# Expert blocks of a mixture of experts: the store of a block's rows moved from the sync engine's queue to ScalarE's

## The chip, the cores and the metric

One core of one Trainium2 chip runs the whole program. The metric is the device time of one execution in microseconds. The program was run three times, and the median is what counts. One execution was also taken with the hardware profiler; its trace is what the text reads.

## The reference, cut to what matters

The reference is one layer of a hybrid backbone over 9 tiles of 128 tokens (1 of a prompt, 8 of a sample): a mixer (attention beside a state-space scan), a mixture of experts, a final norm. Only the experts matter here. Each token takes one group of four experts and in it the two best, so each token is worked on by two experts of 16:

```python
hidden = (jax.nn.silu(jnp.einsum('nd,edf->nef', hf, lw['w_exp_gate']))
          * jnp.einsum('nd,edf->nef', hf, lw['w_exp_up']))
y = jnp.einsum('nef,efd->nd', hidden * combine.astype(hf.dtype)[..., None], lw['w_exp_down'])
```

The model width is 1024, an expert's inner width is 256. So an expert has 2 MB of gate and up weights and 1 MB of down weights in float32.

## The kernel before

**Blocks.** The routing stage sorts the (token, expert) pairs by expert into 33 blocks of 128 rows, each block with one expert (`BLOCKS`). `block_expert`, `block_new` and `block_buf` hold, for each block, its expert, whether that expert differs from the one of the block before, and which of two buffers holds its raw weights. `expert_stage` runs over the blocks: the rows of a block are gathered from HBM (`xg`), turned on TensorE (`x_ps`), split in a high and a low part (`xT_hi`, `xT_lo`), multiplied with gate and up weights that are split in the same way (three matmuls for each product, 24 of 512 columns for a block), passed through SiLU and the routing weight (`hid`), turned and split again (`hidT_hi`, `hidT_lo`), and multiplied with the split down weights (12 matmuls). The result `y_ps` is copied to `y` in SBUF and stored to `y_slots` in HBM, from where the final stage gathers it.

**Engines.** Each engine runs its own `body(t, left)` for each block t. A body works on several blocks at once:

- The sync engine (SP) issues the loads. `load_gu(t+3)` reads three values (expert, buffer, whether new) from SBUF into registers, waits until VectorE has split the gate and up weights of block t+1 (`gu_lo_done`), and issues two loads of 1 MB. Then comes `store(t-1)`: it waits until ScalarE has copied `y` of block t-1 (`y_read`) and issues the store of 512 KB. Then `load_d(t+2)`: three values, a wait for GpSimd's split of block t's down weights, and a load of 1 MB. A load whose expert is not new is skipped (`cond=new`), but it counts on its semaphore.
- ScalarE (ACT) copies the high parts of the turned rows (`x_high`, two halves), does the SiLU, casts the gate and up weights to their high parts in four pieces (`gu_high(t+3)`, two before and two after `evacuate(t)`), evacuates `y_ps` (`evacuate(t)`), and casts the down weights (`d_high(t+2)`). It works in this written order. The first piece of `gu_high(t+3)` waits for the two loads.
- VectorE (DVE) makes the low parts of the gate and up weights, of the rows and of the hidden rows. GpSimd (POOL) makes the low part of the down weights (`d_low`), and issues the gathers.
- TensorE (PE) runs `gate_up(t+1)` in two halves around the turns, and the down product of block t.

`evacuate(t)` waits for the store of the block before: `act.wait_ge(y_out, t.n * 16 + 16)`.

Of the kernel before, what the change touches and what calls it, by code (L numbers as in the profile page):

```python
# [15 lines left out]
P = 128  # L16
# [26 lines left out]
BLOCKS = 2 * TILES + NE - 1  # L43
# [1997 lines left out]
def expert_stage(nc, I, C, W, M):  # L2041
# [5 lines left out]
    with ExitStack() as ctx:  # L2047
# [9 lines left out]
        y = s.sb("y", [P, D])  # L2057
        x_ps, gu_ps, h_ps, y_ps = s.ps("x", D), [s.ps(f"gu{u}") for u in range(2)], s.ps("h"), s.ps("y", D)
        gu_in, d_in, xg_in = ([s.sem(f"{k}{u}") for u in range(2)] for k in ("gu_in", "d_in", "xg_in"))
        y_out = s.sem("y_out")  # L2060
# [5 lines left out]
        hidT_done, y_done, y_read = (s.sem(k) for k in ("hidT_done", "y_done", "y_read"))  # L2066
# [3 lines left out]
        def blocks(eng, body):  # L2070

            assert BLOCKS % 2 == 1
            body(Step(0, 0), 4)
            with eng.Fori(0, (BLOCKS - 5) // 2) as i:
                body(Step(i, 1), 4)
                body(Step(i, 2), 4)
            for n in range(BLOCKS - 4, BLOCKS):
                body(Step(0, n), BLOCKS - 1 - n)

        def weight_buffer(eng, k):  # L2080

            return eng.value_load(W["block_buf"][0:1, bass.ds(k.n, 1)], min_val=0, max_val=1)

        def block_values(eng, k):

            return (eng.value_load(expert[0:1, bass.ds(k.n, 1)], min_val=0, max_val=NE - 1), weight_buffer(eng, k),
                    eng.value_load(W["block_new"][0:1, bass.ds(k.n, 1)], min_val=0, max_val=1))

        @block.sync
        def _(sp):  # L2090
            def load_gu(k):
                e, buf, new = block_values(sp, k)
                sp.wait_ge(gu_lo_done, k.n + 1)
                sp.dma_start(wgu[:, buf, :, 0:FF], I["w_exp_gate"][0, e].rearrange("(k p) f -> p k f", p=P), cond=new).then_inc(gu_in[k.buf], 16)
                sp.dma_start(wgu[:, buf, :, FF:], I["w_exp_up"][0, e].rearrange("(k p) f -> p k f", p=P), cond=new).then_inc(gu_in[k.buf], 16)

            def load_d(k):
                e, buf, new = block_values(sp, k)
                sp.wait_ge(d_lo_done, k.n + 1)
                sp.dma_start(wd[:, buf], I["w_exp_down"][0, e].rearrange("(k p) d -> p k d", p=P), cond=new).then_inc(d_in[k.buf], 16)  # L2100

            def body(t, left):
                if left >= 3:
                    load_gu(t.next().next().next())
                if left == 1:
                    sp.wait_ge(gu_lo_done, BLOCKS + 2)
                    load_final_gains(sp, I, W, M)
                if not (isinstance(t.n, int) and t.n == 0):
                    store(Step(t.i, t.c - 1))
                if left >= 2:  # L2110
                    load_d(t.next().next())

            def store(t):
                sp.wait_ge(y_read, t.n + 2)
                sp.dma_start(M["y_slots"][bass.ds(t.n * P, P), :], y[:]).then_inc(y_out, 16)

            load_gu(Step(0, 0))
            load_d(Step(0, 0))
            load_gu(Step(0, 1))
            load_d(Step(0, 1))  # L2120
            load_gu(Step(0, 2))
            blocks(sp, body)
            store(Step(0, BLOCKS - 1))
            sp.wait_ge(y_out, 16 * (BLOCKS + 1))

        @block.gpsimd
# [94 lines left out]
        @block.scalar  # L2221
        def _(act):
            act.sem_inc(y_read, 1)
            act.sem_inc(y_out, 16)

            def gu_high(k, buf, pieces):
                if pieces[0] == 0:
                    act.wait_ge(gu_in[k.buf], k.nth * 32 + 32)
                    act.wait_ge(gu_done, k.n + 1)
                for j in pieces:  # L2230
                    act.copy(wgu_hi[:, k.buf, j:j + 2], wgu[:, buf, j:j + 2]).then_inc(gu_hi_done, 1)  # L2231

            def d_high(k):
                buf = weight_buffer(act, k)
                act.wait_ge(d_in[k.buf], k.nth * 16 + 16)
                act.wait_ge(y_done, k.n + 1)
                act.copy(wd_hi[:, k.buf], wd[:, buf]).then_inc(d_hi_done, 1)  # L2237

            def x_high(k, half):

                act.wait_ge(x_turned, k.n + 3)
                if half == 0:
                    act.wait_ge(gu_half_done, k.n + 1)
                else:
                    act.wait_ge(gu_done, k.n + 2)
                cols = slice(half * 512, (half + 1) * 512)
                act.copy(xT_hi[:, cols], x_ps[:, cols]).then_inc(x_hi_done[half], 1)

            def silu(k):
                act.wait_ge(gu_done, k.n + 3)  # L2250
                act.wait_ge(hid_done, k.n + 2)
                act.activation(act_g[:], gu_ps[k.buf][:, 0:FF], ACT.Silu).then_inc(silu_done, 1)

            def evacuate(t):
                act.wait_ge(y_done, t.n + 3)
                act.wait_ge(y_out, t.n * 16 + 16)
                act.copy(y[:], y_ps[:]).then_inc(y_read, 1)

            def body(t, left):
                if left >= 2:  # L2260
                    x_high(t.next().next(), 0)
                    x_high(t.next().next(), 1)
                if left >= 1:
                    silu(t.next())
                if left >= 3:
                    ahead = t.next().next().next()
                    buf = weight_buffer(act, ahead)
                    gu_high(ahead, buf, range(0, KT // 2, 2))
                evacuate(t)
                if left >= 3:  # L2270
                    gu_high(ahead, buf, range(KT // 2, KT, 2))
                if left >= 2:
                    d_high(t.next().next())

            gu_high(Step(0, 0), weight_buffer(act, Step(0, 0)), range(0, KT, 2))
            d_high(Step(0, 0))
            x_high(Step(0, 0), 0)
            x_high(Step(0, 0), 1)
            gu_high(Step(0, 1), weight_buffer(act, Step(0, 1)), range(0, KT, 2))
            x_high(Step(0, 1), 0)  # L2280
            x_high(Step(0, 1), 1)
            silu(Step(0, 0))
            gu_high(Step(0, 2), weight_buffer(act, Step(0, 2)), range(0, KT, 2))
            d_high(Step(0, 1))
            blocks(act, body)

        @block.vector
# [56 lines left out]
def load_final_gains(sp, I, W, M):  # L2344
    gate0, gate1, gain = final_gains(W)
    for cond, gate in enumerate((gate0, gate1)):
        sp.dma_start(gate, row_bcast(M["mods"][cond, GATE2 * D:(GATE2 + 1) * D])).then_inc(W["final_in"], 16)
    sp.dma_start(gain, row_bcast(I["final_norm_g"])).then_inc(W["final_in"], 16)
# [229 lines left out]
```

## Time and profile before

| | |
|---|---|
| time, median of 3 runs | 1292.05 us (1291.84 to 1296.66) |
| the profiled execution: time, span | 1293.32 us, 1291.6 us |
| expert stage | from about 880 to 1232 us of the span |
| PE, DVE, ACT, POOL busy over the whole span | 89%, 64%, 51%, 36% |
| stores of `y` | 33 of 512 KB, issued by SP |
| new experts' loads | 2 MB + 1 MB each |

The profile counts an engine as busy while a compute instruction of it runs. The issuing of a DMA, a wait and the reading of a value into a register are not busy time; they stand in the trace under the engine's queue (SPq, ACTq). The granted clock of TensorE is given as a share of its upper level (2.4 GHz); 0.50 is the lower one (1.2 GHz). "DMA share" is the mean busy share of the 16 DMA engines.

### The profile page before, as it was taken

How to read it: one execution, taken by the hardware profiler on the slowest of the kernel's cores; microseconds unless marked ns; L12 is line 12 of the kernel's file. 1: busy time of each engine (PE TensorE's matmuls, PEld its weight loads, DVE VectorE, ACT ScalarE, POOL GpSimd, SP SyncE). 2: the span in 40 equal slices, each digit the busy share in tenths (PEclk: the TensorE clock that was granted, in tenths of full speed). 3: DMA queues.
4: the chain of work that ended last, by engine and by line, in shares of the span. 5: the costliest groups of instructions: out<-in, count | busy, mean ns of one | idle time of the engine just before them, and what ended most of it. 6: DMA issues, size and time to landing. Idle time of an engine off the chain costs nothing. (4 is left out here: it accounts for less than half of the span.)

```text
span 1291.6 us, 19584 instructions
## 1 busy us (share of the span) xinstructions
PE 1149.3 (89%) x6100; PEld 952.6 (74%) x6100; DVE 829.2 (64%) x1234; ACT 658.2 (51%) x1085; POOL 466.3 (36%) x272
## 2 busy tenths in 40 slices
PE   4799999988999996988996999946899989899984
PEld 1687777768999885888886888835678777678751
DVE  0764455014564785777775566667889888999737
ACT  2651112114334773666666455416678787688622
POOL 0000000020001682566772000003687877688650
PEclk9899999989999997999998999967999999999988
DMA  9427586421200907236111533225987987633375
GB/s 365 139 106 278 175 293 220 141 68 38 54 1 3 227 34 168 67 85 147 38 50 47 178 105 101 80 99 194 327 268 259 347 312 252 235 143 115 117 261 210
DMA packets 127093, 204.92 MB, mean 159 GB/s; under 512 B 19265, under 2 KB 89825, under 8 KB 124975
## 3 DMA queue, kind: packets, MB, share of 16 engines
q1 hardware_dynamic: 118108, 176.90, 41.6%
q0 software_dynamic: 7344, 26.74, 6.0%
q10 hardware_dynamic: 1570, 0.38, 0.2%
q8 instruction: 39, 0.64, 0.2%
q14 instruction: 32, 0.25, 0.1%
HBM read 215.61 MB, written 45.01 MB: 202 GB/s over the span
## 5 line engine op out<-in xcount | busy, mean ns | idle before, releaser
L88 DVE TENSOR_TENSOR moe_wgu_lo<-moe_wgu,moe_wgu_hi 128x1024 fp32r<-128x1024 f32 x132 | 222.2, 1720 | 38.7 <-issue 19.8
L88 POOL TENSOR_TENSOR moe_wd_lo<-moe_wd,moe_wd_hi 128x1024 fp32r<-128x1024 f32 x66 | 190.2, 2903 | 62.4 <-ACT moe_wd_hi L2237 61.6
L2231 ACT CAST moe_wgu_hi<-moe_wgu 128x1024 fp32r x132 | 131.7, 1050 | 53.9 <-DMA moe_wgu<-in_w_exp_up 53.5
L93 PE MATMUL proj_acc_ps<-proj_w_hi,hidden_hT_hi 128*128 128x512 f32 x288 | 117.6, 408 | 8.0 <-DVE hidden_hT_lo L88 8.0
L93 PE MATMUL moe_gu_ps<-moe_wgu_hi,moe_xT_hi 128*128 128x512 f32 x264 | 110.6, 419 | 15.5 <-DVE moe_xT_lo L88 15.5
L95 PE MATMUL proj_acc_ps<-proj_w_hi,hidden_hT_lo 128*128 128x512 f32 x288 | 115.2, 400 | 0.0
L94 PE MATMUL proj_acc_ps<-proj_w_lo,hidden_hT_hi 128*128 128x512 f32 x288 | 114.7, 398 | 0.0
L1332 POOL TENSOR_TENSOR att_e<-att_e 128x1152 f32<-128x1152 f32 (+1 forms) x36 | 86.0, 2390 | 77.0 <-DVE att_e L1412 77.0
L94 PE MATMUL moe_gu_ps<-moe_wgu_lo,moe_xT_hi 128*128 128x512 f32 x264 | 106.1, 402 | 0.0
L95 PE MATMUL moe_gu_ps<-moe_wgu_hi,moe_xT_lo 128*128 128x512 f32 x264 | 106.1, 402 | 0.0
L1350 ACT ACTIVATE att_e<-att_sc_ps,att_shift 128x1152 f32<-128x1152 f32 (+1 forms) x72 | 81.5, 1132 | 40.1 <-DVE att_shift L1401 39.9
L719 POOL MEMSET conv_ones<- 128x128 f32 x1 | 0.2, 205 | 280.1 <-POOLq L83 280.1
L1401 DVE TENSOR_REDUCE att_shift<-att_sc_ps 128x1 f32<-128x1152 f32 (+1 forms) x72 | 86.1, 1230 | 5.5 <-PE att_sc_ps L1446 5.3
L1475 PE MATMUL att_turned_ps<-att_in_v_tok,att_aT 128*128 128x128 f32 x584 | 77.2, 280 | 8.2 <-ACT att_aT L1358 8.0
L1475 PEld LDWEIGHTS att_turned_ps<-att_in_v_tok,att_aT 128*128 128x128 f32 x584 | 70.0, 192 | 14.1 <-ACT att_aT L1358 10.8
L93 PEld LDWEIGHTS proj_acc_ps<-proj_w_hi,hidden_hT_hi 128*128 128x128 f32 x288 | 54.8, 190 | 27.5 <-DVE hidden_hT_lo L88 8.2
L93 PEld LDWEIGHTS moe_gu_ps<-moe_wgu_hi,moe_xT_hi 128*128 128x128 f32 x264 | 50.7, 192 | 32.2 <-issue 9.6
L373 ACT ACTIVATE proj_halves<-proj_heads_ps 128x512 fp32r<-128x512 f32 x19 | 11.4, 599 | 106.8 <-PE proj_heads_ps L576 63.4
L93 PE MATMUL conv_group_ps<-hidden_hT_hi,conv_w_hi 128*128 128x384 f32 x192 | 65.1, 339 | 0.0
L95 PEld LDWEIGHTS proj_acc_ps<-proj_w_hi,hidden_hT_lo 128*128 128x128 f32 x288 | 54.8, 190 | 13.2
L2237 ACT CAST moe_wd_hi<-moe_wd 128x2048 fp32r x33 | 63.0, 1908 | 2.6 <-DMA moe_wd<-in_w_exp_down 2.5
L95 PE MATMUL conv_group_ps<-hidden_hT_hi,conv_w_lo 128*128 128x384 f32 x192 | 64.2, 334 | 0.0
(376 smaller groups left out, 2831.2 us busy)
## 6 DMA issues: line engine op xcount, KB each, us to landing
moe_wgu<-in_w_exp_gate SPq DMA_DIRECT2D x34, 1024.0 KB
moe_wgu<-in_w_exp_up SPq DMA_DIRECT2D x34, 1024.0 KB
moe_wd<-in_w_exp_down SPq DMA_DIRECT2D x34, 1024.0 KB
scratch_y_slots<-moe_y SPq DMA_DIRECT2D x33, 512.0 KB
proj_raw<-in_w_in SPq DMA_DIRECT2D x32, 256.0 KB, 5.1
proj_feat<-in_w_ada SPq DMA_DIRECT2D x4, 2048.0 KB, 8.6
proj_xh<-in_w_ada SPq DMA_DIRECT2D x4, 2048.0 KB, 9.9
scratch_h<-late_h SPq DMA_DIRECT2D x9, 512.0 KB, 2.9
```

What stands on the lines that cost most here:

```text
L88: return eng.tensor_tensor(low, value, high.bitcast(F32), ALU.subtract)
L93: pe.matmul(out, a_high, b_high, start=start, stop=False)
L94: pe.matmul(out, a_high, b_low, start=False, stop=False)
L95: return pe.matmul(out, a_low, b_high, start=False, stop=stop)
L373: act.activation(halves[:, m % 2, 0], heads_ps[m % 2][:], ACT.Copy, scale=SCALE if m < TILES else 1.0).then_inc(half_high, 1)
L719: pool.memset(ones[:], 1.0).then_inc(zeroed, 1)
L1332: pool.tensor_tensor(e[:, it.e, 0, 0:it.keys], e[:, it.e, 0, 0:it.keys], e[:, it.e, 1, 0:it.keys], ALU.add).then_inc(a_done, 1)
L1350: act.activation(as_banks(it, e[:, it.e, m, 0:it.keys]), scores_of(it, m), ACT.Exp, bias=shift[:, it.e, m:m + 1], accum_out=total[:, it.e, ...
L1401: dve.tensor_reduce(shift[:, it.e, m:m + 1], scores_of(it, m), AX if it.prompt else AXY, ALU.max, negate=True).then_inc(shift_done[m], 1)
L1475: mm = pe.matmul(o_ps, aT[:, j * P:(j + 1) * P], v_tok[:, j + (0 if it.prompt else 1), it.head * P:(it.head + 1) * P], start=(j == 0), sto ...
L2231: act.copy(wgu_hi[:, k.buf, j:j + 2], wgu[:, buf, j:j + 2]).then_inc(gu_hi_done, 1)
L2237: act.copy(wd_hi[:, k.buf], wd[:, buf]).then_inc(d_hi_done, 1)
```

## The change

`store` leaves the sync engine's body and goes into ScalarE's. There it stands in the body of its own block, behind the last two pieces of `gu_high` and ahead of `d_high`, and it goes through ScalarE's own DMA queue. Its wait on `y_read` now is a wait of ScalarE's sequencer for ScalarE's own copy. The sync engine's body holds only the loads. Nothing of the computation, of the buffers or of the bytes moved is changed.

```diff
@@ expert_stage, block.sync @@
                 if left == 1:
                     sp.wait_ge(gu_lo_done, BLOCKS + 2)
                     load_final_gains(sp, I, W, M)
-                if not (isinstance(t.n, int) and t.n == 0):
-                    store(Step(t.i, t.c - 1))
                 if left >= 2:
                     load_d(t.next().next())
-
-            def store(t):
-                sp.wait_ge(y_read, t.n + 2)
-                sp.dma_start(M["y_slots"][bass.ds(t.n * P, P), :], y[:]).then_inc(y_out, 16)
@@
             load_gu(Step(0, 2))
             blocks(sp, body)
-            store(Step(0, BLOCKS - 1))
             sp.wait_ge(y_out, 16 * (BLOCKS + 1))
@@ expert_stage, block.scalar @@
+            def store(t):
+                act.wait_ge(y_read, t.n + 2)
+                act.dma_start(M["y_slots"][bass.ds(t.n * P, P), :], y[:]).then_inc(y_out, 16)
+
             def body(t, left):
@@
                 evacuate(t)
                 if left >= 3:
                     gu_high(ahead, buf, range(KT // 2, KT, 2))
+                store(t)
                 if left >= 2:
                     d_high(t.next().next())
```

## Rows read from the trace of the kernel before

**Rows 1.** The page, its part 1, TensorE.
```profile
PE 1149.3 (89%) x6100; PEld 952.6 (74%) x6100; DVE 829.2 (64%) x1234; ACT 658.2 (51%) x1085; POOL 466.3 (36%) x272
```
**Rows 2.** Windows of the expert stage: busy us of each engine, granted clock, DMA share, GB/s.
```profile
1000.00:1040.00 40.00, 38.06 (x182) 30.44 (x182) 33.04 (x34) 30.66 (x35) 30.64 (x17) 1.00 0.99 356
1080.00:1120.00 40.00, 33.63 (x151) 26.17 (x150) 35.35 (x30) 26.64 (x31) 29.02 (x16) 0.96 0.68 230
1160.00:1200.00 40.00, 40.00 (x194) 32.47 (x193) 37.79 (x38) 33.93 (x39) 33.77 (x18) 1.00 0.30 111
```
**Rows 3.** Timeline of ACT, evacuations of `y`: first, two of steady blocks, last.
```profile
909.33 1.01 ACT L2257 COPY moe_y<-moe_y_ps 128x1024 f32<-128x1024 f32 x1
...
1149.85 1.02 ACT L2257 COPY moe_y<-moe_y_ps 128x1024 f32<-128x1024 f32 x1
...
1216.43 1.02 ACT L2257 COPY moe_y<-moe_y_ps 128x1024 f32<-128x1024 f32 x1 [1.87 <-PE moe_y_ps L95]
...
1229.34 1.01 ACT L2257 COPY moe_y<-moe_y_ps 128x1024 f32<-128x1024 f32 x1 [3.28 <-PE moe_y_ps L95]
```
**Rows 4.** Waits, 900 to 1232 us, of PE and of ACT: us, times, longest.
```profile
PE moe_gu_ps L93 <- DVE moe_xT_lo L88: 12.5, 8, 3.7
PE moe_y_ps L93 <- DVE moe_hidT_lo L88: 6.2, 9, 1.2
...
ACT moe_wgu_hi L2231 <- DMA moe_wgu<-in_w_exp_up: 29.3, 14, 4.1
...
ACT moe_wd_hi L2237 <- DMA moe_wd<-in_w_exp_down: 2.5, 3, 1.4
```
**Rows 5.** Timeline of SP's queue, 996 to 1012 us: start, us to issue.
```profile
996.89 0.41 SPq L2100 DMA_DIRECT2D moe_wd<-in_w_exp_down  x1
999.68 0.40 SPq L2094 DMA_DIRECT2D moe_wgu<-in_w_exp_gate  x1
1000.29 0.41 SPq L2095 DMA_DIRECT2D moe_wgu<-in_w_exp_up  x1
1001.79 2.81 SPq L2115 DMA_DIRECT2D scratch_y_slots<-moe_y  x1
...
1011.37 0.39 SPq L2094 DMA_DIRECT2D moe_wgu<-in_w_exp_gate  x1
```
**Rows 6.** Timeline of SP's queue, the first and the last long store issue.
```profile
910.51 1.80 SPq L2115 DMA_DIRECT2D scratch_y_slots<-moe_y  x1
...
1121.68 0.87 SPq L2115 DMA_DIRECT2D scratch_y_slots<-moe_y  x1
```
**Rows 7.** The store's line: duration of the issue in ns, min, median, max.
```profile
L2115 SPq DMA_DIRECT2D scratch_y_slots<-moe_y x33: 332/371/3194, 910.5 to 1230.4; - x33
```
**Rows 8.** Waits of SP's queue, 870 to 1240 us.
```profile
SPq L2115 <- ACT moe_y L2257: 66.0, 31, 8.3
SPq L2094 <- DVE moe_wgu_lo L88: 37.6, 19, 5.4
```
**Rows 9.** Timeline of DVE: the split that frees the load at 999.68.
```profile
997.17 1.23 DVE L88 TENSOR_TENSOR moe_wgu_lo<-moe_wgu,moe_wgu_hi 128x1024 fp32r<-128x1024 f32 x1 [0.53 <-issue]
```
**Rows 10.** Timeline of ACT behind a steady block's evacuation.
```profile
1160.26 2.00 ACT L2231 CAST moe_wgu_hi<-moe_wgu 128x1024 fp32r x2
1162.16 1.91 ACT L2237 CAST moe_wd_hi<-moe_wd 128x2048 fp32r x1
...
1166.05 0.59 ACT L2247 CAST moe_xT_hi<-moe_x_ps 128x512 fp32r<-128x512 f32 x1 [1.50 <-PE moe_gu_ps L95]
```
**Rows 11.** Lines 794 and 2082 on ACT's queue: a DMA issue, a value read; ns.
```profile
L794 ACTq DMA_DIRECT2D scratch_sums<-scan_token_rows x2: 335/384/433, 313.9 to 314.3; - x2
L2082 ACTq TENSOR_LOAD <-all_block_buf x66: 273/280/1194, 877.6 to 1216.4; - x66
```
**Rows 12.** DMA issues, GpSimd's gathers of 512 KB: median us to landing.
```profile
moe_xg<-scratch_h,moe_idx POOLq DMA_INDIRECT x31, 5.2
```
**Rows 13.** Window ahead of the down load at 996.89.
```profile
992.00:996.00 4.00, 4.00 (x24) 3.41 (x23) 3.76 (x4) 4.00 (x5) 2.40 (x3) 1.00 0.32 131
```

## The prediction

> **What bounds the kernel now.** I read the page first, for the busy shares: TensorE is busy for 89% of the span [rows 1], so only what lets it idle or slows its clock can be won. Then the windows of the expert stage. In 1160 to 1200, where no expert is new, PE is busy for all of the 40.00 us. In 1000 to 1040, where nearly every block has a new expert, it is busy for 38.06 with the DMA engines at 0.99 and 356 GB/s. In 1080 to 1120 it is busy for 33.63 at a granted clock of 0.96 [rows 2]. So the stage is bound by TensorE in its second half, and by TensorE with some losses in its first.
>
> How large are the losses? The evacuations of `y` mark the blocks. From the first to the last there are 32 intervals in 320.0 us. Seven steady ones take 1216.43 - 1149.85 = 66.58, that is 9.51 each. The last two are shorter because the work runs out (12.91 together). So 30 x 9.51 + 12.91 = 298.2 would do, and 21.8 us are lost [rows 3]. That is the most this stage can give back, 1.7%.
>
> Next the waits. PE waited 12.5 us for the low part of the rows and 6.2 us for the low part of the hidden rows, both VectorE's. ACT, which feeds VectorE, waited 29.3 us in 14 places for gate and up loads, and 2.5 us for down loads [rows 4]. I take it that the loads are the root of the losses: 21.8 us lost for 31.8 us of ACT waiting, 0.69 us for each. (A part may be VectorE and GpSimd getting in each other's way, which the loads only set off.)
>
> Last the queue of SP, as it is where the change acts. It waited 66.0 us for evacuations and 37.6 us for VectorE's splits [rows 8]. The row to see is the stretch from 996.89: the down load is issued, 2.79 us later the gate load of a new expert, then up, then the store, whose issue takes 2.81 us [rows 5].
>
> **What goes from SP.** 33 stores with their waits. Their issues take 0.371 us by the median and up to 3.194 [rows 7]. Thirteen take over 0.7 us, 21.8 us together; each comes within some 3 us of a new expert's loads [rows 5, 6]. I read these as the queue being full behind the loads. What is that worth to the loads?
>
> (a) The gate and up load. It waits for VectorE's split, and its values must have been read, which keeps SP busy for about 2.4 us behind a down load. The split ahead of 999.68 ended at 997.17 + 1.23 = 998.40 [rows 5, 9]. Where SP was already waiting, the issue came 0.4 us behind the split. So this load could go at 998.8, 0.9 us earlier. Of the new experts' loads seven are late by SP in this way (918.88, 939.98, 979.59, 999.68, 1030.63, 1051.65, 1093.80), by 0.8 to 1.8 us, together 7.3. The other seven that ACT waited for gain nothing here.
>
> (b) The down load no longer waits for the evacuation. It follows the gate and up issue by the reading of its values, 2.9 us. It moves earlier by 1 to 5 us, mostly 3. The load at 996.89 would go at about 993.7, into a window where the DMA engines are at 0.32 [rows 13]. Its 1.05 MB are 2.9 us at 356 GB/s [rows 2]. Today a part of this still lies ahead of the gate load, in the same queue. I take 1.0 us for each of the seven loads of (a) (bounds: 0 and 1.6, if a gather of 1.5 us is in between too). The seven others are issued 3.5 us or more behind the down load and gain 0. The 2.5 us of waits for down loads [rows 4] go.
>
> **What comes to ACT.** (c) The issue itself. ACT's own two issues at line 794 take 0.335 and 0.433 us [rows 11]; I take 0.37. Is it hidden? In a steady block the evacuation ends at 1160.37, the issue would run from about 1160.6 to 1160.95, while two casts of 2.00 us run. Behind it on ACT's sequencer stands the value read of `d_high` (0.28 us, with its register work 0.6), done by about 1161.6; the cast of the down weights starts at 1162.16 [rows 10, 11]. So it costs 0, with some 0.5 us of room. Without this room the next cover is the 1.50 us that ACT waits for PE before the second half of the rows [rows 10]. Behind the cast stands GpSimd's `d_low`, and then PE's down product a block later. In blocks where ACT waited for a load, the 1.50 us is gone, but the casts still cover the issue. The bounds are 0 and the case below.
>
> (d) The store's bytes. Today the store stands in SP's queue behind the gate and up loads just issued. On its own queue it runs beside them. The gathers, also on a queue of their own, land in 5.2 us [rows 12], although SP's queue can hold 3 MB, 8.8 us at 356 GB/s; so another queue is served beside the loads, not behind them. The store's 0.52 MB are 1.5 us at that rate. Each store starts 1.5 to 3 us behind a new expert's load, within its flight, and so delays it by up to 1.5 us. In stretches where new experts follow each other without a gap the store of one block lay ahead of the next load anyway, and the delay is not added up. I take 11 of the 14 loads: 16.5 us (bounds 0 and 21).
>
> The Trainium skill (page "DMA: Bandwidth & Descriptors", section "Queues, rings and completion order") has each DMA engine take turns among the queues that have work, a packet at a time. By that rule the full 1.5 us is what (d) costs, as taken. Its section "Issuing engines are not separate DMA queues" speaks against the change: to issue from several engines saves only the sequencer's issue time. By it the sum would be (a) and (b) alone, less (d).
>
> **The sum.** ACT's waits for gate and up loads: -7.3 (a) - 7.0 (b) + 16.5 (d) = +2.2 us, by 0.69 +1.5 us of time. Waits for down loads: -2.5, by 0.69 -1.7. The issue 0. Together -0.2 us. The end of the stage is the same: the last store follows the last evacuation by 0.1 to 0.3 us from either engine. The profiled execution took 1293.32 (span 1291.6 and 1.7 around it), 1.3 above the median of the runs. The difference applied to the median gives 1292 us.
>
> **Rivals.**
>
> *Forecast, no change that can be told* (within 0.5%, 6.5 us, which is about what a measurement of this kernel can tell): chance 0.58. Its own range is 1286 to 1295, from (d) at 8.3 and at its full 21 us.
>
> *Faster: SP's lane counts for more.* If the loads aren't much held up by a store beside them, (d) is near 0, and 14.3 + 2.5 us of waits go, by 0.69 11.6 us: 1280.5. With (d) at 5 us it is 8 us: 1284. For it speaks that in 1000 to 1040 some slack in PE is tied to these very waits, and that the idle DMA window ahead of the down load would be used [rows 13]. Against it: several of the 14 waits are below 1 us, and can't give more than they are. It decides when (d) stays under 7 us. Chance 0.23.
>
> *Slower: the issue stalls ACT as it stalled SP.* If the 0.76 to 3.19 us are not the fullness of SP's own queue but something that both queues share, ACT's sequencer is held in the same 13 blocks for 21.8 us. Less 0.9 us each for the issue and the room that covers it, 10.1 us fall on the casts of the down weights, in blocks where ACT is late already: by 0.69 7 us, and with the sum above 1299. For it: the long issues all follow loads [rows 5, 6]. Against: ACT's few issues that the trace shows are short, though no full queue stood beside them [rows 11]. It decides from a mean issue of about 1.5 us in these blocks. Chance 0.10.
>
> *Slower: the store holds up every load.* (d) is at 21 us, (a) and (b) bring only half, 7, and the waits for down loads stay: ACT's waits grow by 14 us, by 0.69 9.7 us: 1302. Chance 0.09.
>
> *The change does nothing at all*, as the loads were bound by bandwidth and by VectorE's splits: within the first.
>
> From these: faster 0.23, same 0.58, slower 0.19. The range from 1283 to 1300 leaves out the far end of the faster case and of the second slower one, about 2 in 10.
>
> **What would show it.** SP's queue in the profile after: the down load about 2.9 us behind the up load, seven of the gate loads 0.9 us nearer to their split, and SP's wait for VectorE grown from 37.6 to near 100 us. ACT's queue: 33 issues of the store, 0.33 to 0.45 us each; some above 1 us would mean the first slower case. ACT's wait for gate and up loads: about 31 us; under 20 is the faster case, over 40 the second slower one. The wait for down loads gone. Steady blocks of 9.51 us, as before; if they are longer, the issue was not hidden. The prediction is wrong if the losses of 21.8 us don't follow ACT's waits, but the moments at which VectorE and GpSimd meet, which every shift of 1 us can turn either way; the total of the losses then moves by several us with no change in the waits.

## The result, and the profile after

Slower, by 1.1%: 1307.93 us median of 6 runs (1302.72 to 1311.88), against 1292.96 (1291.84 to 1296.66) for the kernel before. The ratio is 1.0107, with a 95% interval of 1.0082 to 1.0133. I had forecast 1292.0 and a range up to 1300; both are wrong. The profiled execution took 1303.68 us (span 1301.9), 10.4 more than that of before. So the traces show 10.4 of the 15.0 us.

First the waits of ACT and PE in the expert stage (us, times, longest), which answer to [rows 4]:

```profile
PE moe_gu_ps L93 <- DVE moe_xT_lo L88: 19.3, 9, 3.6
PE moe_y_ps L93 <- DVE moe_hidT_lo L88: 5.9, 8, 1.0
```
```profile
ACT moe_wgu_hi L2224 <- DMA moe_wgu<-in_w_exp_up: 28.0, 13, 3.4
ACT moe_xT_hi L2240 <- PE moe_x_ps L2169: 14.2, 6, 3.9
...
ACT moe_y L2250 <- DMA scratch_y_slots<-moe_y: 2.0, 2, 1.1
```

ACT waits for the gate and up loads about as long as before (28.0 us against 29.3), and no longer for down loads. By the account of my prediction the time should not have moved. But PE waits 19.3 us for the low part of the rows, where it waited 12.5.

The evacuations of `y`, from ACT's timeline, answer to [rows 3]:

```profile
910.86 1.00 ACT L2250 COPY moe_y<-moe_y_ps 128x1024 f32<-128x1024 f32 x1
...
972.77 1.00 ACT L2250 COPY moe_y<-moe_y_ps 128x1024 f32<-128x1024 f32 x1
987.03 1.02 ACT L2250 COPY moe_y<-moe_y_ps 128x1024 f32<-128x1024 f32 x1
...
1169.73 1.01 ACT L2250 COPY moe_y<-moe_y_ps 128x1024 f32<-128x1024 f32 x1
...
1179.32 1.02 ACT L2250 COPY moe_y<-moe_y_ps 128x1024 f32<-128x1024 f32 x1
...
1239.74 1.01 ACT L2250 COPY moe_y<-moe_y_ps 128x1024 f32<-128x1024 f32 x1 [3.28 <-PE moe_y_ps L95]
```

From the first to the last it is 328.9 us instead of 320.0. Less the 298.2 of the prediction, 30.7 us are lost where 21.8 were. A steady block still takes about 9.5 us (1179.32 - 1169.73 = 9.59). The lost time is in single blocks: six intervals are 14.1 to 14.3 us long, such as 987.03 - 972.77. The kernel before has one that is longer than 13.2 us (16.0).

The windows say the same. Here is 940 to 1000, after and then before (span of the window, busy us of PE, PEld, DVE, ACT and POOL, granted clock, DMA share, GB/s):

```profile
940.00:1000.00 60.00, 53.59 (x252) 43.10 (x252) 49.99 (x51) 40.71 (x47) 43.49 (x23) 0.97 0.69 230
```
```profile
940.00:1000.00 60.00, 59.29 (x285) 48.01 (x284) 53.96 (x57) 50.01 (x57) 48.34 (x25) 1.00 0.77 265
```

PE is busy 5.7 us less there, every other engine too, and the DMA engines move less. No engine and no bandwidth has become the bound; something is waited for.

The store's issue on ACT, the counterpart of [rows 7] (ns, min, median, max), and one steady block behind its evacuation, the counterpart of [rows 10]:

```profile
L2254 ACTq DMA_DIRECT2D scratch_y_slots<-moe_y x33: 338/343/396, 911.9 to 1240.8; - x33
```
```profile
1169.73 1.01 ACT L2250 COPY moe_y<-moe_y_ps 128x1024 f32<-128x1024 f32 x1
1170.64 1.05 ACT L2224 CAST moe_wgu_hi<-moe_wgu 128x1024 fp32r x1
1170.91 0.34 ACTq L2254 DMA_DIRECT2D scratch_y_slots<-moe_y  x1
1171.60 1.05 ACT L2224 CAST moe_wgu_hi<-moe_wgu 128x1024 fp32r x1
1172.55 1.90 ACT L2230 CAST moe_wd_hi<-moe_wd 128x2048 fp32r x1
```

No issue takes over 0.40 us, and the casts run on without a gap. SP's queue is as forecast too. Here are a new expert's gate and up loads with the down load's issue 2.8 us behind (0.09 us, as its expert isn't new and it is skipped), which answer to [rows 5], and SP's wait for VectorE between 870 and 1245, which answers to [rows 8]:

```profile
940.91 0.39 SPq L2094 DMA_DIRECT2D moe_wgu<-in_w_exp_gate  x1
941.52 0.42 SPq L2095 DMA_DIRECT2D moe_wgu<-in_w_exp_up  x1
944.31 0.09 SPq L2100 DMA_DIRECT2D moe_wd<-in_w_exp_down  x1
```
```profile
SPq L2094 <- DVE moe_wgu_lo L88: 119.9, 30, 7.4
```

Does the store cut into these loads? The packets of the DMA queues show it (q1 is SP's, q10 is ACT's; packets, MB, and the time the packets took as a share of 16 engines' time, which can pass 100% where packets overlap). First 946 to 948.5 in the kernel after, with the store that ACT issued at 941.45; then the same length, 947.5 to 950, in the kernel of experiment 1 below, where the store stands behind the loads:

```profile
q1 hardware_dynamic: 484, 0.48, 54.4%
q10 hardware_dynamic: 143, 0.52, 51.2%
```
```profile
q1 hardware_dynamic: 929, 0.93, 106.6%
```

In these 2.5 us the store takes about half of the packets' time, and the loads move 0.48 MB instead of 0.93. In sum it is much the same (1.00 MB and 0.93), so the second queue brings next to no bandwidth here.

**Where a lost block comes from.** The timelines of VectorE, GpSimd and PE around 970 to 976:

```profile
969.58 5.42 DVE L88 TENSOR_TENSOR moe_wgu_lo<-moe_wgu,moe_wgu_hi 128x1024 fp32r<-128x1024 f32 x1 [0.44 <-issue]
974.92 1.27 DVE L88 TENSOR_TENSOR moe_xT_lo<-moe_x_ps,moe_xT_hi 128x512 fp32r<-128x512 f32 x2
```
```profile
969.19 4.72 POOL L88 TENSOR_TENSOR moe_wd_lo<-moe_wd,moe_wd_hi 128x1024 fp32r<-128x1024 f32 x2
```
```profile
975.83 0.79 PE L93 MATMUL moe_gu_ps<-moe_wgu_hi,moe_xT_hi 128*128 128x512 f32 x1 [3.57 <-DVE moe_xT_lo L88]
976.41 0.63 PE L94 MATMUL moe_gu_ps<-moe_wgu_lo,moe_xT_hi 128*128 128x512 f32 x1
...
979.58 0.39 PE L94 MATMUL moe_gu_ps<-moe_wgu_lo,moe_xT_hi 128*128 128x512 f32 x1
```
```profile
976.00:980.00 4.00, 4.00 (x12) 3.16 (x13) 4.00 (x5) 1.47 (x1) 3.17 (x2) 0.65 0.60 157
```

VectorE's last piece of the weights takes 5.42 us where the same piece took 1.23 [rows 9]. It began 0.4 us behind GpSimd's first piece of `d_low` and ended 1.1 us behind the end of the second. So it seems to have done its work after both. The low part of the rows stands behind it, and PE was idle for 3.57 us. After this PE ran its matmuls in 0.63 instead of 0.39 us for some 2.5 us. The window from 976 to 980 has a granted clock of 0.65, so part of it ran at 1.2 GHz and part at 2.4. I call such an instruction, a piece of over 5 us, a *long hold*. The longest other pieces take 3.5 us, about one piece of GpSimd's and their own time. The kernel before has one long hold, and the kernel after three:

```profile
1101.67 5.37 DVE L88 TENSOR_TENSOR moe_wgu_lo<-moe_wgu,moe_wgu_hi 128x1024 fp32r<-128x1024 f32 x1 [0.53 <-issue]
...
1107.92 0.47 PE L93 MATMUL moe_gu_ps<-moe_wgu_hi,moe_xT_hi 128*128 128x512 f32 x1 [3.65 <-DVE moe_xT_lo L88]
```
```profile
1036.46 5.43 DVE L88 TENSOR_TENSOR moe_wgu_lo<-moe_wgu,moe_wgu_hi 128x1024 fp32r<-128x1024 f32 x1 [0.43 <-issue]
...
1133.28 5.33 DVE L88 TENSOR_TENSOR moe_wgu_lo<-moe_wgu,moe_wgu_hi 128x1024 fp32r<-128x1024 f32 x1 [0.52 <-issue]
```

Each of the four is followed by a PE gap of 3.56 to 3.65 us and by 6 or 7 slowed matmuls. That accounts for the 10.3 us between the two spans. PE's wait for the rows grows by 6.8 us (19.3 - 12.5), and two more such gaps are 7.1. PE is busy 328.4 us in the stage (880 to 1243) where it was 324.9 (880 to 1233), for the same 1518 matmuls: 3.5 us for more slowed ones. A long block need not have a hold, though. Three of the six intervals of 14 us come right behind one; in the other three (from 940.27, 1007.17 and 1103.94) PE waits 1.2 to 2.0 us for the rows, and no piece in them or in the block before takes over 3.5 us.

The Trainium skill (page "SBUF — State Buffer", section "Who interferes with whom") says that a VectorE instruction with two SBUF inputs contends with a GpSimd instruction that reads SBUF, that what they share is an exclusive lock, and that the order of issue decides who blocks. The trace fits that for a single piece: at 926.49 of the kernel after, one took 3.06 us that began 0.42 behind a piece of GpSimd's. That the waiting one can lose twice in a row, as here, the page does not say.

So two things need an explanation: why the gate and up loads did not come earlier with a lane of their own, and what turns lateness into losses.

### The profile page after: what moved, and what is told of

Same layout as the page of the kernel before. It is cut to its first block and busy times, and to the rows that moved or that the text cites. A ratio compares the mean times of both kernels' runs of the same rounds, so it can differ in the third digit from the quotient of the medians.

```text
span 1301.9 us, 19584 instructions
## 1 busy us (share of the span) xinstructions
PE 1153.3 (89%) x6100; PEld 955.2 (73%) x6100; DVE 834.8 (64%) x1234; ACT 657.9 (51%) x1085; POOL 464.5 (36%) x272
## 5 line engine op out<-in xcount | busy, mean ns | idle before, releaser
L88 DVE TENSOR_TENSOR moe_wgu_lo<-moe_wgu,moe_wgu_hi 128x1024 fp32r<-128x1024 f32 x132 | 227.3, 1758 | 40.1 <-ACT moe_wgu_hi L2224 23.8
L93 PE MATMUL moe_gu_ps<-moe_wgu_hi,moe_xT_hi 128*128 128x512 f32 x264 | 112.0, 424 | 21.7 <-DVE moe_xT_lo L88 21.7
L1475 PEld LDWEIGHTS att_turned_ps<-att_in_v_tok,att_aT 128*128 128x128 f32 x584 | 70.0, 192 | 14.0 <-ACT att_aT L1358 10.8
L93 PEld LDWEIGHTS moe_gu_ps<-moe_wgu_hi,moe_xT_hi 128*128 128x128 f32 x264 | 51.5, 195 | 37.6 <-issue 12.5
L2240 ACT CAST moe_xT_hi<-moe_x_ps 128x512 fp32r<-128x512 f32 x66 | 37.9, 586 | 53.6 <-PE moe_gu_ps L95 36.2
L95 PEld LDWEIGHTS proj_acc_ps<-proj_w_hi,hidden_hT_lo 128*128 128x128 f32 x288 | 54.8, 190 | 13.2
```

The costliest lines, as they stand in the source:

```text
L88: return eng.tensor_tensor(low, value, high.bitcast(F32), ALU.subtract)
L93: pe.matmul(out, a_high, b_high, start=start, stop=False)
L95: return pe.matmul(out, a_low, b_high, start=False, stop=stop)
L1475: mm = pe.matmul(o_ps, aT[:, j * P:(j + 1) * P], v_tok[:, j + (0 if it.prompt else 1), it.head * P:(it.head + 1) * P], start=(j == 0), sto ...
```

## The experiments

In every verdict "before" is the kernel before, run on the same chip, and the ratio is to it. Experiments 1, 2 and 6 ran on one chip, 3, 4 and 7 on a second, 8 and 9 on a third, 5 on a fourth; the median of the kernel before was 1293.6, 1296.5, 1293.5 and 1293.9 us there. So from one experiment to another the ratios say more than the times. Waits and long holds are those of the one profiled execution. "Down load first" is experiment 1's kernel.

**1. Down load first, store left on SP.**

```diff
                     load_final_gains(sp, I, W, M)
-                if not (isinstance(t.n, int) and t.n == 0):
-                    store(Step(t.i, t.c - 1))
                 if left >= 2:
                     load_d(t.next().next())
+                if not (isinstance(t.n, int) and t.n == 0):
+                    store(Step(t.i, t.c - 1))
```

> The store stays on the sync engine, but behind the down load instead of ahead of it, so the down load goes early as in the changed kernel and the store's bytes stay in the loads' queue. Theory A (the store's bytes on a queue of their own hold up the gate and up loads): within 3 us of before, 1290 to 1296. Theory B (the early down load is what shifts the order of things): slower like the changed kernel, 1303 to 1310. Theory C (ScalarE's wait and issue): as A.

Measured: 1286.49 us (1283.81 to 1292.2), ratio 0.9953 (0.9929 to 0.9976): 7 us faster than before, and below the range of each of my theories, of which A was the nearest. It takes the earlier down load from the change and leaves the store's queue as it was. Its waits:

```profile
ACT moe_y L2257 <- DMA scratch_y_slots<-moe_y: 14.3, 5, 3.3
ACT moe_wgu_hi L2231 <- DMA moe_wgu<-in_w_exp_up: 7.9, 10, 1.7
```
```profile
PE moe_gu_ps L93 <- DVE moe_xT_lo L88: 6.9, 7, 2.0
```

The gate and up waits fall by 21.4 us. The store now lands late and the next evacuation waits 14.3 us for it. From the first to the last evacuation it is 1222.58 - 910.79 = 311.8 us, so 13.6 are lost: whatever this wait costs is within them.

**2. The change, with the down load as late as before.** A wait and a mark on a spare semaphore in the store's old place on SP.

```diff
                     load_final_gains(sp, I, W, M)
+                if not (isinstance(t.n, int) and t.n == 0):
+                    sp.wait_ge(y_read, t.n + 1)
+                    sp.sem_inc(passed, 1)
                 if left >= 2:
```

> The changed kernel, but the sync engine still waits for the evacuation of the block before, ahead of the down load. The store is ScalarE's. Theory A: as slow as the changed kernel, 1303 to 1310. Theory B: back to before, 1290 to 1296. Theory C: as A.

Measured: 1308.75 us (1305.72 to 1313.0), ratio 1.0118 (1.0084 to 1.0151), gate and up waits 31.7 us in 12 places. The slowdown is there in full, without the earlier down load, as theory A had it. So the store on ACT's queue makes it. It also shows that with the store there, the earlier down load is worth too little to be told.

**3. Is it the issue on ACT, or the bytes?** Down load first, and ACT also issues a store of 8 KB to a spare place, with its waits.

```diff
+            def store(t):
+                act.wait_ge(y_read, t.n + 2)
+                act.dma_start(M["y_spare"][bass.ds(t.n * P, P), :], y[:, 0:16]).then_inc(spare_out, 16)
```

> As the run with the down load first (store on the sync engine behind the down load, 1286.5), and beside it ScalarE waits for its own evacuation and issues a store at the changed kernel's place, but of 8 KB to a scratch tensor instead of 512 KB. Theory A (the bytes on a second queue): within 3 us of 1286.5. Theory C (ScalarE's sequencer is held by the wait and the issue): 1303 or more.

Measured: 1286.51 us (1283.35 to 1291.04), ratio 0.9943 (0.9917 to 0.997), waits 8.8 us. That its median is experiment 1's to 0.02 us is chance, as the chips differ, but the ratios agree within their intervals too: the issue, its wait and a queue of its own cost nothing that can be told. The bytes remain.

**4. Half of the bytes.** Down load first, ACT stores columns 0 to 511, SP the rest behind the down load.

```diff
-                sp.dma_start(M["y_slots"][bass.ds(t.n * P, P), :], y[:]).then_inc(y_out, 16)
+                sp.dma_start(M["y_slots"][bass.ds(t.n * P, P), 512:], y[:, 512:]).then_inc(y_out, 16)
...
+                act.dma_start(M["y_slots"][bass.ds(t.n * P, P), 0:512], y[:, 0:512]).then_inc(y_out, 16)
```

> As the run with the down load first, but the store is cut in two: ScalarE stores the first 512 columns from its queue at the changed kernel's place, the sync engine the other 512 behind the down load. Theory A: between the two, 1291 to 1303, about 1297. Theory C: as slow as the changed kernel, 1304 to 1310, since ScalarE's wait and issue are the same.

Measured: 1300.52 us (1292.1 to 1307.77), ratio 1.0049 (1.0021 to 1.0077), waits 20.0 us. With 0, 256 and 512 KB a block on ACT's queue the time is 1286.5, 1300.5 and 1307.9, and the waits are 7.9, 20.0 and 28.0: both rise with the bytes. As ratios the three are 0.9953, 1.0049 and 1.0107. This kernel's profiled execution, of which the waits are, took 1292.10 us and was the fastest of 12, so in a usual one they may be longer.

**5. An extra store of 512 KB, on either queue.** Down load first, and `y` goes to a spare place as well, from ACT (at the change's place) or from SP (behind the first store). The next evacuation waits for it.

```diff
+                act.dma_start(M["y_spare"][bass.ds(t.n * P, P), :], y[:]).then_inc(spare_out, 16)
```
```diff
                 sp.dma_start(M["y_slots"][bass.ds(t.n * P, P), :], y[:]).then_inc(y_out, 16)
+                sp.dma_start(M["y_spare"][bass.ds(t.n * P, P), :], y[:]).then_inc(spare_out, 16)
```

> The run with the down load first (1286.5), and beside it a second store of the same 512 KB to a scratch tensor from ScalarE's queue, at the changed kernel's place; nothing left out. Theory A (bytes on a queue of their own reach into the flight of the gate and up loads): at least as slow as the changed kernel, 1303 to 1325, with ScalarE's waits for these loads at 25 us or more. If only the queue of the real store mattered: 1286 to 1292.

> The run with the down load first, with the same second store of 512 KB on the sync engine's queue, right behind the first. The same bytes as in the run beside it. Theory A: the loads that the stores stand behind are not held up, ScalarE's waits for gate and up loads stay under 15 us; what grows is its wait for the stores before the evacuation: 1288 to 1300, at least 10 us below the run beside it. If the bytes cost whatever the queue: within 5 us of the run beside it.

Measured: on ACT 1316.7 us (1310.69 to 1319.7), ratio 1.0157 (1.0112 to 1.0201); on SP 1314.22 (1308.81 to 1314.83), ratio 1.0132 (1.0091 to 1.0174). On ACT it is as theory A had it. On SP theory A is missed, and the time is what the rival had forecast, that the bytes cost whatever the queue: the two are 2.5 us apart. The waits do separate the queues. With the extra store on ACT, then on SP:

```profile
ACT moe_wgu_hi L2232 <- DMA moe_wgu<-in_w_exp_up: 29.1, 12, 4.0
ACT moe_y L2260 <- DMA scratch_y_slots<-moe_y: 14.6, 6, 3.8
```
```profile
ACT moe_y L2261 <- DMA scratch_y_spare<-moe_y: 43.9, 21, 4.9
...
ACT moe_wgu_hi L2233 <- DMA moe_wgu<-in_w_exp_up: 9.5, 8, 2.9
```

The same bytes hold up the loads by 21.2 us from ACT's queue (29.1 - 7.9) and by 1.6 from SP's, behind the loads. There they land late instead, and with one buffer for `y` that became the evacuation's wait. Neither profiled execution has a long hold; the longest of these VectorE pieces takes 3.5 us. So a kernel can lose 20 us and more against experiment 1 without any.

**6. GpSimd's split cut to 16 columns of each half**, once in the kernel after and once in the one before, to take away the meetings with VectorE. The first two blocks keep it whole.

```diff
-                    op = split_low(pool, wd_lo[:, k.buf, half], wd[:, buf, half], wd_hi[:, k.buf, half])
+                    c = slice(0, D if full else 16)
+                    op = split_low(pool, wd_lo[:, k.buf, half, c], wd[:, buf, half, c], wd_hi[:, k.buf, half, c])
```

> The changed kernel, with GpSimd's split of the down weights cut from 1024 to 16 columns of each half (in all blocks but the first two; the low parts of the others are stale, so the output is not the reference's). Theory D (what costs is that VectorE's splits are held by GpSimd's, and the change only moves which ones meet): the losses nearly go and this kernel and the same cut of the kernel before are within 3 us of each other, both 15 us or more below before. Theory A without D: it stays 8 us or more above the same cut of before.

> The kernel before with the same cut of GpSimd's split (output not the reference's for the same reason). Theory D: 1270 to 1278, within 3 us of the changed kernel with the cut. Otherwise 8 us or more below that one.

Measured: the change with the cut 1283.05 us (1278.03 to 1286.81), ratio 0.9911 (0.9879 to 0.9943); before with it 1277.04 (1275.33 to 1282.36), ratio 0.9879 (0.9847 to 0.9912). The gap shrinks from 15 to 6 us. That is neither of my forecasts: theory D wanted 3 us or less and both at least 15 below before (the change is 10 below), A without D 8 or more. ACT's waits for gate and up loads are longer than in either whole kernel, with the change and then without:

```profile
ACT moe_wgu_hi L2225 <- DMA moe_wgu<-in_w_exp_up: 40.0, 14, 5.0
```
```profile
ACT moe_wgu_hi L2232 <- DMA moe_wgu<-in_w_exp_up: 36.4, 14, 3.5
```

Yet both are faster than before. PE's wait for the rows' low part is 1.5 us in both. So ACT's waits do not set the time at a fixed rate; more than half of the change's price needs GpSimd's long splits. The cut takes away every meeting with VectorE, the short ones and the long holds alike, so it doesn't say which of them cost. What is left of the price shows as PE's wait for the hidden rows' low part: 10.8 us with the change, 5.6 without.

**7. Shorter pieces on GpSimd.** Four pieces of 512 columns instead of two of 1024, on experiment 1 and on the change. If a hold lasts as long as GpSimd's piece, shorter ones should help.

```diff
-                for half in range(2):
-                    op = split_low(pool, wd_lo[:, k.buf, half], wd[:, buf, half], wd_hi[:, k.buf, half])
+                for piece in range(4):
+                    half, c = piece // 2, slice(piece % 2 * 512, piece % 2 * 512 + 512)
+                    op = split_low(pool, wd_lo[:, k.buf, half, c], wd[:, buf, half, c], wd_hi[:, k.buf, half, c])
```

> As the run with the down load first, with GpSimd's split of the down weights in four pieces of 512 columns instead of two of 1024; nothing left out. Theory D (VectorE is held behind a whole piece of GpSimd's): VectorE waits for shorter pieces, 1278 to 1284. If the holding follows GpSimd's whole work and not a piece, no change: 1285 to 1288, or a little more for four starts.

> The changed kernel with GpSimd's split in four pieces. Theory D: the long holds of 5.4 us, which take both pieces, get rarer or shorter, 1292 to 1302. Otherwise as the changed kernel, 1303 to 1310.

Measured: 1311.04 us (1308.38 to 1315.87), ratio 1.0134 (1.0096 to 1.0172), and 1318.59 (1316.75 to 1324.62), ratio 1.0195 (1.0156 to 1.0234). A clear miss: both are above all my ranges. With the first kernel's gate and up waits at 6.4 us, there are five long holds like this one, and steady blocks are longer as well (VectorE's three pieces come every 10.13 us):

```profile
1077.83 5.68 DVE L88 TENSOR_TENSOR moe_wgu_lo<-moe_wgu,moe_wgu_hi 128x1024 fp32r<-128x1024 f32 x1 [0.44 <-issue]
...
1168.89 5.34 DVE L88 TENSOR_TENSOR moe_wgu_lo<-moe_wgu,moe_wgu_hi 128x1024 fp32r<-128x1024 f32 x3
1179.02 5.35 DVE L88 TENSOR_TENSOR moe_wgu_lo<-moe_wgu,moe_wgu_hi 128x1024 fp32r<-128x1024 f32 x3
```

A hold is as long with four pieces as with two, so its length isn't that of one piece: VectorE can be held over a whole run of them. And these 25 us came with hardly a late load.

**8. A one-column GpSimd copy ahead of the split**, on the change and on experiment 1, in case the long hold depends on GpSimd's split following its gather directly.

```diff
                 buf = weight_buffer(pool, k)
+                pool.tensor_copy(pad[:, bass.ds(k.n, 1)], token[:, 0:1])
                 pool.wait_ge(d_hi_done, k.n + 1)
```

> The changed kernel, with one copy of a single column on GpSimd between a gather and the split of the down weights that follows it; nothing left out. Theory E (the long holds of VectorE, 5.3 to 5.8 us, arise only where GpSimd's split starts at once behind its gather and VectorE's hidden-row split has just ended; each costs the kernel some 5 us, and the changed kernel has more of them since its loads land later): no long holds in the trace, and the time falls by most of what they cost, to 1285 to 1295. If the holds are only a matter of when the two engines meet: as the changed kernel, 1303 to 1310.

> The run with the down load first (1286.5, no long hold in its trace), with the same copy. Theory E: there is nothing to take away, 1285 to 1289. With the changed kernel plus the copy, the difference of the two is what the later landing costs without the long holds: 2 to 8 us.

Measured: 1311.73 us (1307.89 to 1315.26), ratio 1.0138 (1.0105 to 1.0172), with five long holds; and 1288.45 (1283.85 to 1292.84), ratio 0.9956 (0.9936 to 0.9977), with none. The copy doesn't take the holds away: this theory of the trigger falls. The first is 2 us above the range of the plain rival, the second in the range given.

**9. VectorE's rows first.** Down load first, the first half of the rows' low part ahead of VectorE's last piece of the weights.

```diff
                 if left >= 2:
+                    x_low(t.next().next(), (0,))
                     gu_low(t.next().next(), range(KT - 2, KT, 2))
-                    x_low(t.next().next())
+                    x_low(t.next().next(), (1,))
```

> The run with the down load first, with VectorE making the low part of the first half of the rows ahead of its last piece of gate and up weights, not behind it. VectorE's request for that piece then comes 0.7 us later and TensorE's wait for the rows ends sooner: 1280 to 1286 if the holds behind GpSimd's split are what TensorE waits for, and no long hold. If the piece is itself what TensorE waits for: 1286 to 1292.

Measured: 1290.54 us (1286.99 to 1293.03), ratio 0.9973 (0.9952 to 0.9993). No better than experiment 1, whose gate and up waits it raises from 7.9 to 21.7 us. PE now waits 8.6 us for the piece of the weights and no longer for the rows: the expectation's second case. Experiment 1 has no long hold to take away, so this run doesn't test whether the order shields PE from one.

**Long holds against time**, my count in the one profiled execution of each kernel with whole splits:

| kernel (experiment) | long holds | gate and up waits, us | profiled, us |
|---|---|---|---|
| small store on ACT (3) | 0 | 8.8 | 1284.91 |
| down load first (1) | 0 | 7.9 | 1286.51 |
| the same, spacer (8) | 0 | 11.9 | 1287.51 |
| rows first (9) | 0 | 21.7 | 1291.01 |
| half on each (4) | 0 | 20.0 | 1292.10 |
| before | 1 | 29.3 | 1293.32 |
| the change | 3 | 28.0 | 1303.68 |
| down load as before (2) | 4 | 31.7 | 1308.99 |
| the change, spacer (8) | 5 | 31.7 | 1310.34 |
| down load first, four pieces (7) | 5 | 6.4 | 1312.06 |
| the change, four pieces (7) | 8 | 22.1 | 1318.82 |
| extra store on SP (5) | 0 | 9.5 | 1313.98 |
| extra store on ACT (5) | 0 | 29.1 | 1316.04 |

Without the last two rows the order by holds is the order by time. The order by waits nearly is too, as long as GpSimd works in two pieces; the four-piece kernels break it. The last two break the order by holds: they are among the slowest and have none. So the holds account for the step from before to the change, but are not the only way in which late transfers cost time.

## Why the prediction was wrong, by its own steps

**(a) and (b), loads earlier: right in kind, too small.** I took -7.3 and -7.0 us of ACT's waits. Experiment 1, which has the earlier down load and no bytes beside the loads, shows -21.4 (SP still waits 16.3 us for evacuations in it, so (a) is not wholly in it). I had left the seven other waits of [rows 4] untouched, and (b) was put at 1.0 us a load; by that run -14.3 should have been about -21.4. The waits for down loads went, as said.

**(c), the issue: right.** 0.343 us by the median, hidden; steady blocks unchanged; experiment 3 prices it at nothing. The rival in which the issue stalls ACT falls: none of the 33 took over 0.40 us. That SP's long issues [rows 6, 7] were the fullness of its own queue fits this, but no run isolates it. A term was missing: with one buffer for `y`, ACT now waits 2.0 us for the store in 2 places.

**(d), the store's bytes: right in kind, somewhat small.** From experiment 1 to the change the waits rise by 28.0 - 7.9 = 20.1 us in 13 places, 1.5 each. On average that is the size I took for one, but in all of them instead of 11 of 14; 16.5 should have been 20.1. Both rules of the Trainium skill's page "DMA: Bandwidth & Descriptors" that the prediction weighed fit the packets shown above. By the turns among queues of the Trainium skill's section "Queues, rings and completion order" the store should take its share beside the loads: its packets took 51.2% of the engines' time, the loads' 54.4%. By the Trainium skill's section "Issuing engines are not separate DMA queues" it should bring no bandwidth: 1.00 MB moved, against 0.93. The single turns are not shown. So the second lane only let the store in ahead of bytes of loads that had been issued first.

The errors of the two terms cancel, which is luck: their sum is -1.3 us, where I had +2.2. **The step that failed is the conversion**, 0.69 us of time for a us of ACT's wait. It was drawn from one trace, as if the 21.8 us lost were made by the 31.8 waited. With 1.3 us less waiting, 8.9 us more are lost. Experiments 6 and 7 break it in both directions: longer waits with less time, and 6.4 us of waits with 25 us more time. Counted as in the prediction (time lost between the first and the last evacuation, per us that ACT waits for transfers), it is 0.69 before, 0.61 in experiment 1, 1.02 with the change, 0.19 in experiment 6 on the kernel before and 1.6 in experiment 7 on the down load first. What the change added is the price of meetings between VectorE and GpSimd. The prediction named this as what would make it wrong, but gave it no price and no chance. One row, the 5.37 us piece at 1101.67, would have given the price: 3.65 us of PE idle there, and a slower clock behind it. Two more such holds, some 5 us each, are the 10.4 us between the profiled executions. The other 4.6 us of the 15.0 between the medians lie in executions of which there is no trace.

The rivals: "holds up every load" forecast a time of 1302, near the 1307.93 measured, but by waits 14 us longer, which are not there; its (d) of 21 us is what was measured, its (a) and (b) are not. "Faster" is what the down load alone does. Taken in this order, the change is a gain of about 7 us (down load ahead of the store) and a loss of about 21 (the store off SP's queue; 1307.93 against 1286.49, or 20 by the ratios). In the other order the gain isn't there: by experiment 2 the earlier down load is worth under 1 us once the store is on ACT's queue.

**Shown and open.** Shown: the store's bytes on a second queue, at the place where ACT issues them, make the slowdown (experiments 2 to 4), hold up the gate and up loads (4, 5), and more than half of the price needs GpSimd's long splits (6). Not separated: the queue and the moment. On ACT's queue the store starts within the flight of the loads; a later issue from ACT, behind them, was not tried. Read from the traces, but not isolated: that late loads bring the long holds about by moving VectorE's last piece into the start of GpSimd's split. In the kernels with two pieces they come only with gate and up waits of 28 us and more; but the extra store on ACT has 29.1 us of waits and no long hold, and four pieces bring them without late loads. How that kernel loses its time without them is open. What exactly makes VectorE lose to GpSimd's second piece too stays open, after two theories that fell (7, 8). To start 0.4 us behind GpSimd's first piece isn't enough: the piece at 926.49 did so and took 3.06 us. A second buffer for `y`, which would free experiment 5 on SP and experiment 1 from the wait for the store, was not tried.

The best version is experiment 1's, 1286.49 us, ahead of both kernels.

## What to carry to other kernels

A store behind the loads in their own queue leaves them alone, and costs nothing as long as its buffer isn't wanted before it has landed; on a queue of its own it takes its share out of the loads in flight. Before a transfer is given its own lane, ask whether what it stood behind was more urgent, and change the order within the queue first. And do not turn waits into time by a ratio from one trace: find the blocks in which the time is lost and price the one instruction that loses it.

## What the runs showed of the hardware

- VectorE's split of 1024 columns (1.23 us alone) sometimes took 5.3 to 5.9 us (6.5 once, in the change with four pieces), and then ended about 1.1 us behind the last of GpSimd's consecutive pieces, two of 2.4 us or four of about 1.3 us. In most of these cases GpSimd's first piece had begun 0.3 to 0.6 us before it, but other pieces that began so took about 3 us.
- A PE gap of 3.57 us was followed by matmuls of 0.63 instead of 0.39 us, with a granted clock of 0.65 over 976 to 980 us, the 4 us behind it. A gap of 1.96 us (ending at 1008.67 in the kernel after) was followed by matmuls of 0.63 us too; the same gap in experiment 1 was not.
- Store issues on SP's queue took up to 3.19 us behind loads [rows 7], while those on ACT's queue stayed under 0.40. With the stores gone, SP's own issues were short too (0.60 us at most from 905 to 1209), so no run shows an issue on ACT's queue while SP's is full.
- Within 2.5 us (946 to 948.5 in the kernel after) the packets of a store on ACT's queue took 51.2% of the DMA engines' time and moved 0.52 MB, those of the loads on SP's queue 54.4% and 0.48 MB.
